# A convolution block worked on by single channel chunks, with the convolved chunks added up on VectorE

## What is computed

```python
def conv_module(h, w_pw1, w_dw, b_dw, ln_g, ln_b, w_pw2):
    u = h @ w_pw1                                # 1024 -> 2048
    a, gate = jnp.split(u, 2, axis=-1)
    u = a * jax.nn.sigmoid(gate)
    u = lax.conv_general_dilated(                # depthwise over time, 31 taps
        u, w_dw[:, None, :].astype(u.dtype), window_strides=(1,),
        padding=[(CONV_PAD, CONV_PAD)], dimension_numbers=('NWC', 'WIO', 'NWC'),
        feature_group_count=D_MODEL) + b_dw
    u = jax.nn.silu(layer_norm(u, ln_g, ln_b))   # over the 1024 channels
    return u @ w_pw2
```

## Time and profile before

| | |
|---|---|
| median of three runs | 1512.65 us (1510.72 to 1512.73) |
| profiled execution | 1512.73 us, span 1510.9 us |
| TensorE busy | 1434.8 us, 95% of the span |
| VectorE busy | 945.1 us, 63% |
| ScalarE busy | 584.9 us, 39% |
| mean granted TensorE clock | 0.98 |
| stretch of the module that the diff touches | about 591 to 740 us of the span |

### The profile page before, as it was taken

One profiled execution on the slowest core, in us unless ns is written; L12 is line 12 of the kernel. 1 busy time (PEld: TensorE's weight loads), 2 busy tenths in 40 slices (PEclk: granted clock), 3 DMA queues, 4 the chain that ended last, 5 costly groups with the idle time before them and its releaser, 6 DMA issues.

```text
span 1510.9 us, 24508 instructions
## 1 busy us (share of the span) xinstructions
PE 1434.8 (95%) x10544; PEld 1246.0 (82%) x10544; DVE 945.1 (63%) x1127; ACT 584.9 (39%) x704; POOL 390.5 (26%) x302
## 2 busy tenths in 40 slices
PE   5888999989999999999899999999999998899999
PEld 5887899979999997764477888888886965899998
DVE  7877665466768666866637777256415578586343
ACT  5623445443334364210624222332223457433433
POOL 4975603000003400000002343442330010034553
PEclk9999999989999999999899999999999999999999
DMA  8532324555666465975426655334333400475552
GB/s 264 170 119 90 113 88 144 202 181 190 228 226 234 168 223 179 256 217 139 149 77 218 207 168 167 126 128 163 115 111 112 167 29 2 140 223 170 193 171 82
DMA packets 159540, 239.64 MB, mean 159 GB/s; under 512 B 6960, under 2 KB 129872, under 8 KB 159312
## 3 DMA queue, kind: packets, MB, share of 16 engines
q1 hardware_dynamic: 154640, 233.11, 47.2%
q10 hardware_dynamic: 4800, 5.08, 1.4%
HBM read 227.55 MB, written 1.05 MB: 151 GB/s over the span
## 4 chain that ended last, share of the span: by engine, by line
PE 85%; DVE 8%; ACT 3%; issue 2%; DMA 1%; SPq 0%; POOL 0%; DVEq 0%; ACTq 0%; POOLq 0%
PE bank L2087 25%; PE bank L2088 25%; PE bank L2089 25%; PE bank L2397 2%; DVE wlo L1144 1%; PE bank L2151 1%; PE bank L2565 1%; ACT whi L681 1%; PE bank L2554 1%; PE bank L2239 1%; DVE stat L1826 1%; PE bank L2276 1%; DVE A L1297 1%; PE bank L609 1%; PE bank L590 1%
## 5 line engine op out<-in xcount | busy, mean ns | idle before, releaser
L2087 PE MATMUL bank<-ahi,whi 128*128 128x256 f32 (+1 forms) x2480 | 795.2, 321 | 29.0 <-POOL alo L625 7.6
L2088 PE MATMUL bank<-alo,whi 128*128 128x256 f32 (+1 forms) x2480 | 786.4, 317 | 0.0
L2089 PE MATMUL bank<-ahi,wlo 128*128 128x256 f32 (+1 forms) x2480 | 785.9, 317 | 0.0
L681 ACT ACTIVATE whi<-raw 128x2048 fp32r<-128x2048 f32 x160 | 306.3, 1915 | 720.1 <-PE bank L2089 720.1
L1144 DVE TENSOR_TENSOR wlo<-raw,whi 128x2048 fp32r<-128x2048 f32 x160 | 367.1, 2295 | 346.6 <-ACT whi L681 346.2
L2087 PEld LDWEIGHTS bank<-ahi,whi 128*128 128x128 f32 x2480 | 480.0, 194 | 73.0 <-issue 33.5
L2089 PEld LDWEIGHTS bank<-ahi,wlo 128*128 128x128 f32 x2480 | 479.9, 194 | 28.9
L2088 PEld LDWEIGHTS bank<-alo,whi 128*128 128x128 f32 x2480 | 480.4, 194 | 27.7 <-issue 0.2
L2054 POOL TENSOR_TENSOR A<-A 128x512 f32 (+1 forms) x48 | 106.8, 2238 | 482.8 <-ACT A L1010 482.8
L2036 POOL TENSOR_TENSOR alo<-A,ahi 128x512 fp32r<-128x512 f32 (+1 forms) x43 | 126.5, 2945 | 353.8 <-ACT ahi L884 353.8
L1508 DVE SCALAR_TENSOR_TENSOR A<-modraw,scc,A 128x1024 f32<-128x1024 f32 x70 | 121.3, 1772 | 0.6
(11 more groups left out here) (301 smaller groups left out, 1195.2 us busy)
## 6 DMA issues: line engine op xcount, KB each, us to landing
raw<-in_w_ff SPq DMA_DIRECT2D x64, 1024.0 KB, 5.2
modraw<-in_w_mod SPq DMA_DIRECT2D x72, 512.0 KB, 4.5
raw<-in_w_in SPq DMA_DIRECT2D x28, 1024.0 KB, 5.2
A<-in_w_mod SPq DMA_DIRECT2D x24, 512.0 KB, 4.7
raw<-in_pw SPq DMA_DIRECT2D x12, 1024.0 KB, 7.4
raw<-in_w_ffn_gate SPq DMA_DIRECT2D x11, 1024.0 KB, 5.3
raw<-in_w_ffn_up SPq DMA_DIRECT2D x11, 1024.0 KB, 5.3
raw<-in_w_ffn_down SPq DMA_DIRECT2D x11, 1024.0 KB, 5.2
```

Source lines behind the costliest of these rows:

```text
L681: act.activation(whi[:, k % 2, :], raw[:, kk, :], ACT.Copy).then_inc(whi_ready, 1)
L2087: pe.matmul(out_, w_hi, a_hi, start=start, stop=False, **kw)
L2088: pe.matmul(out_, w_hi, a_lo, start=False, stop=False, **kw)
L2089: return pe.matmul(out_, w_lo, a_hi, start=False, stop=stop, **kw)
```

## The change

One block of pw1 now holds one chunk of `a` and its chunk of `gate` (the matrix is reordered on the host), and all that follows goes chunk by chunk. After block l come one sigmoid, one product, 16 copies of one chunk, issued half by ScalarE and half by SyncE. On ScalarE the sigmoid and the copies now stand ahead of `ahead(p)`, and `mod_rows(2)`, `mod_rows(3)` behind it. On VectorE the taps of chunk l-1 alternate with the last taps of chunk l-2, `ahead` of the block before stands among them, and the last chunks' taps run alone. TensorE convolves chunk l-2 behind block l, from l = 2 on; blocks use PSUM banks 0 to 3 in place of 0 to 5. `chunk_added(c)` sums the convolved chunks 0 to 6 on VectorE into `csum`, so that TensorE sums two tiles (`seven_sum`, `channel_sum(7)`) in place of eight. The turn and the last four mod pieces move behind the mean, `store_mods` behind the reciprocal, an early `Sqrt` on one column loads ScalarE's root table before the squares. SyncE loads the taps of one chunk at a time and the blocks of weights behind the copies.

```diff
+        csum = area(9984, 512)
...
-                return cols(I["pw1"], (D if odd else 0) + 256 * p.h, 256)
+                return cols(I["pw1"], 256 * l, 256)
...
-        def shift_copies(eng, h, j0):
+        def shift_copies(eng, c, j0):
+
+            eng.wait_ge(u_ready, c + 1)
+            if c >= 2:
+                eng.wait_ge(shifted_landed[c % 2], 256 * (c // 2))
+            if c >= 4:
+                eng.wait_ge(conv_done, c - 3)
             for j in (j0, j0 + 1):
                 for q in range(4):
-                    eng.dma_start(shifted[32 * j:32 * j + 32, h % 2, q, :, :, :],
-                                  stage[32 * q:32 * q + 32, h % 2, :, :, j:j + SHIFTW])\
-                       .then_inc(shifted_landed[h % 2], 16)
+                    eng.dma_start(shifted[32 * j:32 * j + 32, c // 2 % 2, q, c % 2, :, :],
+                                  stage[32 * q:32 * q + 32, c // 2 % 2, c % 2, :, j:j + SHIFTW])\
+                       .then_inc(shifted_landed[c % 2], 16)
 
         @block.sync
...
-                    for c in range(4):
-                        load_taps(c)
+                    load_taps(0)
                     for l in range(8):
+                        shift_copies(sync, l, 2)
                         if 1 <= l <= 5:
                             load_mod(22 + 2 * l)
                             load_mod(23 + 2 * l)
-                        if l < 2:
-                            load(name, Pos(FIRST[name] + 6 + l, 6 + l))
-                        elif l < 6:
-                            load("pw2", Pos(FIRST["pw2"] + l - 2, l - 2))
-                        if l in (4, 6):
-                            load_taps(l)
+                        if l < 7:
                             load_taps(l + 1)
-                        if l % 2:
-                            sync.wait_ge(u_ready, l + 1)
-                            if l >= 5:
-                                sync.wait_ge(conv_done, l - 3)
-                            shift_copies(sync, l // 2, 2)
+                        if 1 <= l < 3:
+                            load(name, Pos(FIRST[name] + 5 + l, 5 + l))
+                        elif 3 <= l < 7:
+                            load("pw2", Pos(FIRST["pw2"] + l - 3, l - 3))
...
-            return 2 * (l % 3)
+            return 2 * (l % 2)
...
-            def copies(h):
-
-                act.wait_ge(u_ready, 2 * h + 2)
-                if h >= 2:
-                    act.wait_ge(conv_done, 2 * h - 2)
-                shift_copies(act, h, 0)
-
             def act_pw1(p):
-                h = p.least // 2
+                l = p.least
+                act.wait_ge(block_done, p.b + 1)
+                if l >= 2:
+                    act.wait_ge(u_ready, l - 1)
+                act.activation(sgc[:, l % 2, :], pb[pw1_bank(l) + 1][:, :], ACT.Sigmoid).then_inc(sig_ready, 1)
+                shift_copies(act, l, 0)
                 ahead(p)
-                if p.least == 3:
-                    mod_rows(2)
-                if p.least % 2:
-                    act.wait_ge(block_done, p.b + 1)
-                    for m in range(2):
-                        n = p.l - 1 + m
-                        if n >= 2:
-                            act.wait_ge(u_ready, n - 1)
-                        act.activation(sgc[:, m, :], pb[pw1_bank(p.least) + m][:, :], ACT.Sigmoid).then_inc(sig_ready, 1)
-                    if p.least == 7:
-                        mod_rows(3)
-                    copies(h)
+                if l in (3, 7):
+                    mod_rows(2 + l // 7)
 
             each_block(act, "pw1", act_pw1, roll=False)
+            act.activation(stat[:, 50:51], epsb, ACT.Sqrt)
...
+            tap_end = {}
+
+            def tap(c, k):
+
+                if k == 0 and c == 0:
+                    dve.wait_ge(vtaps_landed, 16)
+                w = vtaps[:, VTAPS * c + k:VTAPS * c + k + 1]
+                src_ = stage[:, c // 2 % 2, c % 2, :, VTAP0 + k:VTAP0 + k + T1]
+                if k == 0:
+                    dve.wait_ge(u_ready, c + 1)
+                    i = dve.tensor_scalar(cacc[:, c, :, :], src_, w, C["convb"][:, c:c + 1], ALU.mult, ALU.add)
+                else:
+                    dve.wait_ge(tap_added, tap_end[c])
+                    i = dve.scalar_tensor_tensor(cacc[:, c, :, :], src_, w, cacc[:, c, :, :], ALU.mult, ALU.add)
+                i.then_inc(tap_added, 1)
+                added[0] += 1
+                tap_end[c] = added[0]
 
             def convolved(c):
 
                 dve.wait_ge(conv_done, c + 1)
-                dve.wait_ge(tap_added, 2 * VTAPS * (c // 2 + 1))
+                dve.wait_ge(tap_added, tap_end[c])
                 dve.tensor_tensor(cacc[:, c, :, :], cacc[:, c, :, :],
                                   pb[4 + c % 2][:, :].rearrange("p (s t) -> p s t", s=2), ALU.add).then_inc(conv_out, 1)
 
...
+            def chunk_added(c):
+
+                if c == 0:
+                    return
+                dve.wait_ge(conv_out, c + 1)
+                if c >= 2:
+                    dve.wait_ge(chunks_added, c - 1)
+                dve.tensor_tensor(csum, cacc[:, 0, :, :].rearrange("p s t -> p (s t)") if c == 1 else csum,
+                                  cacc[:, c, :, :].rearrange("p s t -> p (s t)"), ALU.add).then_inc(chunks_added, 1)
+
+            def conv_input(c):
+
+                if c == 0:
+                    dve.wait_ge(pad_ready, 1)
+                if c >= 4:
+                    dve.wait_ge(shifted_landed[c % 2], 256 * (c // 2 - 1))
+                dve.wait_ge(sig_ready, 15 + c + 1)
+                dve.tensor_tensor(stage[:, c // 2 % 2, c % 2, :, 15:15 + T1],
+                                  sgc[:, c % 2, :].rearrange("p (s t) -> p s t", s=2),
+                                  pb[pw1_bank(c)][:, :].rearrange("p (s t) -> p s t", s=2),
+                                  ALU.mult).then_inc(u_ready, 1)
+
+            for l in range(8):
+                p = Pos(FIRST["pw1"] + l, l)
+                if l == 0:
                     final_norm()
-                ahead(p)
-
-            each_block(dve, "pw1", dve_pw1, roll=False)
-            dve.wait_ge(u_ready, 8)
-            taps_of(3, 0, 3)
-            convolved(4)
-            taps_of(3, 3, 6)
-            convolved(5)
-            taps_of(3, 6, VTAPS)
-            convolved(6)
+                else:
+                    for k in range(6):
+                        if l >= 2 and k < VTAPS - 6:
+                            tap(l - 2, 6 + k)
+                        tap(l - 1, k)
+                        if k == 3:
+                            ahead(Pos(p.b - 1, l - 1))
+                if l >= 3:
+                    convolved(l - 3)
+                    chunk_added(l - 3)
+                if l == 7:
+                    for k in range(6, VTAPS):
+                        tap(6, k)
+                conv_input(l)
+            ahead(p)
+            for k in range(VTAPS):
+                if k == 4:
+                    convolved(5)
+                    chunk_added(5)
+                if k == 10:
+                    convolved(6)
+                    chunk_added(6)
+                tap(7, k)
             convolved(7)
-            store_mods(0, 4, 2, 2, 7)
-
             dve.wait_ge(msum_done, 1)
             for u in range(KD):
                 cu = cacc[:, u, :, :].rearrange("p s t -> p (s t)")
                 dve.scalar_tensor_tensor(cu, pb[0][:, :], -1.0 / D, cu, ALU.mult, ALU.add).then_inc(cen_ready, 1)
             dve.wait_ge(lstd_ready, 1)
             dve.reciprocal(rstd[:, 0:128], rstd[:, 0:128]).then_inc(lrstd_ready, 1)
+            store_mods(0, 4, 2, 2, 7)
             dve.wait_ge(lspread_done, 1)
...
-                if l >= 3:
-                    pe.wait_ge(u_ready, 2 * ((l - 3) // 2 + 1))
-                if l == 5:
-                    pe.wait_ge(conv_out, 2)
+                if l >= 2:
+                    pe.wait_ge(u_ready, l - 1)
...
-                if m == 0:
-                    pe.wait_ge(shifted_landed[r], 256 * (c // 4 + 1))
-                if c in (0, 2):
-                    pe.wait_ge(u_ready, 4 + c)
+                pe.wait_ge(shifted_landed[m], 256 * (c // 2 + 1))
...
+            def seven_sum():
+                pe.wait_ge(chunks_added, KD - 2)
+                pe.matmul(pb[0][:, :], C["ones"], csum, start=True, stop=False)
+
             def channel_sum(c):
                 pe.wait_ge(conv_out, c + 1)
-                return pe.matmul(pb[0][:, :], C["ones"], cacc[:, c, :, :], start=(c == 0), stop=(c == KD - 1))
+                return pe.matmul(pb[0][:, :], C["ones"], cacc[:, c, :, :], start=False, stop=True)
 
             for l in range(8):
                 pw1_block(l)
-                if l in (4, 6):
-                    convolve(l - 4)
-                    convolve(l - 3)
+                if l >= 2:
+                    convolve(l - 2)
                 if l == 4:
                     mod_turn(2)
                 if 1 <= l < 7:
```

(65 more changed lines are left out.)

## The result

The changed kernel takes 1516.23 us in the median of 12 runs (1514.43 to 1519.17), the kernel before, run beside it, 1512.29 (12 runs, 1510.48 to 1514.24): a ratio of 1.0024, 95% interval 1.0017 to 1.0031. It is 3.9 us slower. The profiled execution took 1516.74 us, with a span of 1514.9, 4.0 above that of before.

A forecast was written before the change was run, and what follows sets the result against it. TensorE, busy for 95% of the span, was taken to bound the kernel. Terms 1.6 + 2.6 + 2.4 + 0.1 - 0.6 = +6.1 us on 1512.65 gave 1518.8 us, range 1509 to 1525.

The forecast's parts named there:

- rival 3: TensorE's clock stays up behind the hole at l = 3: 6.1 less 2.4, so 1516.4 us; chance 0.15.
- The price of an issue: Each 71 KB copy holds its issuing queue 0.68 us, so 5.4 us for a chunk's eight (bounds 3.0 and 6.6).
- Rivals 1 and 2: Issues cheap for smaller copies (1508.3 us, chance 0.13); issues that do not hold ScalarE (1503 us, chance 0.04).
- (a) Block 2: TensorE's pw1 block 2 waits for lo, late behind ScalarE's issues and hi: +1.6 us (bounds 0 and 2.7).
- (b) The mod row: At l = 3 TensorE's mod piece waits for mod_rows(2): hole of 4.9 us in place of 2.3, +2.6 us.
- (c) The clock: Behind the l = 3 hole TensorE runs at half clock for 4.3 to 5.8 us: +2.4 us (bounds 0 and 3.0).
- (d) The tail: From pw1's last block to the complete mean, VectorE ends last: 4.4 + 25.75 - 30.1 = +0.1 us (bounds -3.7, +5.4).
- (e) The early Sqrt: ScalarE's root table load of 1.28 us moves to where it waits: -0.6 us (bounds -1.2 and +0.5).
- Rival 4: Crowded queues: both queues start together beside weight loads, eight issues take 6.6 to 8 us; 1525 to 1528 us, chance 0.15.

The follow-up runs named there:

- seventh experiment: Changed kernel with hi and mod row ahead of the copies at every block, then eight channel sums back on TensorE, VectorE additions gone: 1504.77 us, ratio 0.9945.
- the first experiment: Changed kernel with mod_rows(2) put ahead of block 3's sigmoid and copies on ScalarE: 1509.31 us, ratio 0.9979 to the kernel before.
- the fifth experiment: Kernel before the change, with mod_rows(2) put ahead of block 3's hi: 1508.80 us, ratio 0.9980 to the unedited kernel before.
- the sixth: Changed kernel with ten filler matmuls on constants on TensorE behind convolve(1) at l = 3: 1515.09 us, ratio 1.0020 to the kernel before.
- the third experiment: Changed kernel with VectorE's last lo of the stage put behind chunk 7's taps and evacuation: 1508.72 us, ratio 0.9986 to the kernel before.
- the fourth experiment: Changed kernel with all 16 copies of a chunk issued by SyncE, none by ScalarE: 1506.18 us, ratio 0.9963 to the kernel before.

## Why the prediction was right, and where it was off

The prediction forecast slower by 6.1 us; it is slower by 3.9, inside the range, by the mechanism of the forecast. By the number alone one could not tell: 1516.2 is rival 3's 1516.4, and only the profile, where the clock does fall, says that the forecast's terms are all there, with the clock's too large and the tail's too. Step by step:

- **The price of an issue** (0.68, eight 5.4): 5.42 to 5.47 at six of the blocks, 7.20 and 6.76 at two. The median of 0.636 that I took for 142 KB is that of one set, the shortest; and the bound of 0.82 is one set's mean too; over all 32 on ScalarE the median is 0.676 and the mean 0.88, against 0.626 and 0.73 for 71 KB. So the least price is the same for both sizes (0.59 and 0.60), but the typical one is lower for the smaller copies. Rivals 1 and 2 (cheap issues, or issues that don't hold ScalarE) are refuted by the same rows: hi starts 0.1 us behind the last issue each time. By the Trainium skill (Perfetto Trace Analysis, DMA Instruction — HWDGE) a sequencer is free only at the end of an issue's window; the rows agree. Its other rule (same page, DMA Optimizations), that splitting may let some work start sooner, has something for it once the order is mended: convolution and tail then take 4.4 + 17.5 = 21.9 us against 30.1 before. The additions on VectorE have 3 us of that (seventh experiment); how the rest divides no run here shows.
- **(a) Block 2**, +1.6: the hole is 1.58, at 604.59 where 604.6 was forecast.
- **(b) The mod row**, +2.6: 4.72 in place of 2.33, so +2.4; the first and the fifth experiment show that this hole is end time whole.
- **(c) The clock**, +2.4: this is the mis-sized term. The clock did fall to the lower level, but came back 3 us behind the hole, not 4.3 to 5.8, and 1.5 us were lost. I took the length of the slow stretch from two holes elsewhere in the kernel; here it was shorter than behind either. That the 1.5 us reached the end in the changed kernel rests on the first experiment; the sixth regained the clock and not the time. Rival 3 (the clock stays up) is refuted.
- **(d) The tail**, +0.1: 4.4 + 25.2 - 30.1 = -0.5. Within it the steps hold: product 7 at T(7)+2.7 (+2.8 forecast), VectorE 7.5 us idle before lo (7.45), the last convolution held for 7.3 us (7.4), then at half clock for its first 5.5 us and still no later than the taps. Its cause is shown by the third experiment.
- **(e) The early Sqrt**, -0.6: from centring to the reciprocal 6.5 us (730.08 to 736.56), before it was 7.25 (its reciprocal started at 732.47), so -0.8.

The sum of the measured terms is 1.6 + 2.4 + 1.5 - 0.5 - 0.8 = +4.2, the shift of the second pointwise convolution's first matmul is 4.1, the span's 4.0. Of the 2.2 us between forecast and median, the clock is 0.9, the tail 0.6, hole and Sqrt 0.2 each; the rest is spread. Rival 4 (crowded queues) appeared at blocks 4 and 5, where the loop had 2.6 us to spare and nothing waited for it.

One thing the sum could not show: I treated T(7) as the point from which the tail counts. The sixth experiment's profile shows that product 7 hangs on the chain from product 6 through issues, hi and lo, so a term ahead of T(7) isn't sure to reach the end.

## What to carry to other kernels

A copy from SBUF to SBUF holds the queue of the engine that issues it for at least 0.59 us here, for 16 KB, 71 KB or 142 KB alike, so splitting transfers costs issue time: for the same bytes ScalarE issued for 28.3 us before and 46.6 after, SyncE for 33.6 and 43.6. Before doing it, list what stands behind the issues on that engine, and put what others wait for ahead of them. Going second, behind short work that was ready, cost the copies nothing; going first, they made what stood behind them wait: in block 7 hi starts at T(7)+8.3 in place of T(7)+0.5. When a change moves the bound to another engine, look at the order on that engine before judging the change: the same edit is +0.24% with the issues first and -0.7% with them second.

## What the runs showed of the hardware

- The order on ScalarE is not symmetric: issues of DMAs began 0.9 us into a running activation of 1.90 (694.55 and 695.48 above), while an activation behind issues started only after the last, at all eight blocks.
- TensorE's granted clock came back about 3 us behind a hole of 4.7 us, against 4.3 and 5.8 us behind holes of 5.0 and 3.9, 5.5 behind the hole of 7.3 and 5.8 behind the fourth experiment's 4.5; the length of the slow stretch did not follow from the length of the hole. Matmuls on constants that filled the hole (4.58 us of work, 0.21 left idle) kept it at 2.4 GHz.
- The same eight issues took 5.42 to 7.20 us in one profile. The first set took 5.42 with the DMA engines at 278 GB/s, the longest 7.20 at 142; the cause is open.
- A table load of 1.28 us put ahead of the wait for the squares' input ran at 715.31, with nothing but the Sqrt on one column behind it until 730.80; the next one, behind the root, still comes (736.54).
